# A two-block transformer kernel: what loads and runs behind the first weight units, and a new order in its attention stages

## What is computed

```python
h = rmsnorm(x, attn_norm_g)
qa, ka, va, qb, kb, vb = split(h @ w_in)       # widths 512 128 128 512 512 512
qa = apply_axial_rope(rmsnorm(qa, a_q_norm_g)) # 8 heads of 64
ka = apply_axial_rope(rmsnorm(ka, a_k_norm_g)) # 2 heads of 64
out_a = softmax(qa @ ka.T * scale) @ va        # grouped queries, "a"
qb = rmsnorm(qb, b_q_norm_g); kb = rmsnorm(kb, b_k_norm_g)
p = softmax(qb @ kb.T * scale + rel_bias[bucket])        # 4 heads x 2 parts, "b"
ob = (p[0] - lam * p[1]) @ vb                  # lam from four vectors of 64
x = x + concat(out_a, rmsnorm(ob) * c) @ w_out
x = x + square(relu(rmsnorm(x, mlp_norm_g) @ w_up)) @ w_down
```

## Time and profile before

| | us |
|---|---|
| runs before | 1024.4, 1025.13, 1030.17 (median 1025.13) |
| profiled execution | 1021.25 |
| its span | 1019.9 |
| PE busy in it | 982.2 (96%) |
| DVE busy | 721.9 (71%) |
| ACT busy | 521.2 (51%) |
| POOL busy | 56.8 (6%) |
| granted TensorE clock, mean | 0.99 |

### The profile page before, as it was taken

The page is one execution under the profiler, slowest core; times in us unless marked ns, Lnnn a source line. Parts: engine busy times, 40 slices in busy tenths (PEclk is TensorE's granted clock), DMA queues, the critical chain, the costliest instruction groups (busy, mean ns, idle before and its releaser), DMA issues.

```text
span 1019.9 us, 12867 instructions
## 1 busy us (share of the span) xinstructions
PE 982.2 (96%) x4772; PEld 808.6 (79%) x4772; DVE 721.9 (71%) x1073; ACT 521.2 (51%) x805; POOL 56.8 (6%) x64
## 2 busy tenths in 40 slices
PE   6999789999999999999989999999988989999998
PEld 5877578888888888888878888888877868888887
DVE  4865667889776777777767987797666866656653
ACT  5555555555345544444457755456464564444531
POOL 2211100000000000000000022030100000000000
PEclk7999999999999999999999999999999999999999
DMA  7742237888887688778755766786542628764761
GB/s 242 219 157 81 87 122 235 273 270 290 295 300 275 207 251 257 227 237 294 280 141 180 250 198 191 253 304 213 178 134 103 218 100 269 237 201 135 257 205 52
DMA packets 116204, 214.64 MB, mean 210 GB/s; under 512 B 8786, under 2 KB 16234, under 8 KB 115886
## 3 DMA queue, kind: packets, MB, share of 16 engines
q1 hardware_dynamic: 115790, 213.53, 64.1%
q0 software_dynamic: 64, 0.07, 0.2%
q10 hardware_dynamic: 288, 0.23, 0.1%
HBM read 212.71 MB, written 2.13 MB: 211 GB/s over the span
## 4 chain that ended last, share of the span: by engine, by line
PE 87%; DVE 6%; ACT 2%; DMA 2%; issue 1%; SPq 1%; POOL 0%; ACTq 0%; DVEq 0%
PE ps L1149 26%; PE ps L1151 26%; PE ps L1150 26%; PE ps L1199 3%; PE ps L1241 2%; DVE wlo L1817 2%; PE ps L1274 1%; DMA raw<-in_w_mix 1%; PE ps L1255 1%; DMA early<-in_w_in 1%; PE ps L1177 1%; DVE qkT L2256 1%; ACT fP L1609 1%; PE ps L1339 1%; PE ps L1341 1%
## 5 line engine op out<-in xcount | busy, mean ns | idle before, releaser
L1455 ACT ACTIVATE whi<-raw 128x1024 fp32r<-128x1024 f32 (+1 forms) x306 | 313.5, 1031 | 311.2 <-PE ps L1151 201.0
L1817 DVE TENSOR_TENSOR wlo<-raw,whi 128x1024 fp32r<-128x1024 f32 (+1 forms) x306 | 359.6, 1189 | 115.3 <-ACT whi L1455 113.0
L1149 PE MATMUL ps<-whi,hTh 128*128 128x512 f32 (+1 forms) x832 | 327.5, 394 | 8.4 <-DVE wlo L1817 4.0
L1151 PE MATMUL ps<-whi,hTl 128*128 128x512 f32 (+1 forms) x832 | 317.1, 381 | 0.0
L1150 PE MATMUL ps<-wlo,hTh 128*128 128x512 f32 (+1 forms) x832 | 316.9, 381 | 0.0
L1149 PEld LDWEIGHTS ps<-whi,hTh 128*128 128x128 f32 x832 | 157.2, 189 | 39.0 <-DVE wlo L1817 5.2
L1151 PEld LDWEIGHTS ps<-whi,hTl 128*128 128x128 f32 x832 | 157.1, 189 | 30.9
L1150 PEld LDWEIGHTS ps<-wlo,hTh 128*128 128x128 f32 x832 | 157.6, 189 | 27.5 <-issue 0.5
L2162 DVE SCALAR_TENSOR_TENSOR aacc<-araw,cs,aacc 128x512 f32<-128x512 f32 x126 | 95.1, 754 | 2.5
L2402 POOL TENSOR_TENSOR stat<-stat,mhalf 128x8 f32<-128x8 f32 (+3 forms) x29 | 35.9, 1249 | 639.3 <-DVE stat L1833 471.4
L1149 PE MATMUL ps<-whi,uh_ffn 128*128 128x512 f32 x176 | 69.3, 394 | 0.0
(11 more groups left out here) (244 smaller groups left out, 1071.9 us busy)
## 6 DMA issues: line engine op xcount, KB each, us to landing
raw<-in_ffn_w_in SPq DMA_DIRECT2D x80, 512.0 KB, 4.4
araw<-in_w_ada SPq DMA_DIRECT2D x72, 512.0 KB, 5.0
raw<-in_w_mix SPq DMA_DIRECT2D x64, 512.0 KB, 4.6
raw<-in_ffn_w_out SPq DMA_DIRECT2D x44, 512.0 KB, 4.7
raw<-in_w_up SPq DMA_DIRECT2D x32, 512.0 KB, 4.6
raw<-in_w_down SPq DMA_DIRECT2D x32, 512.0 KB, 5.1
raw<-in_w_out SPq DMA_DIRECT2D x16, 512.0 KB, 3.9
raw<-in_w_in SPq DMA_DIRECT2D x14, 512.0 KB, 6.1
```

The source lines that it names most:

```text
L1149: pe.e.matmul(o, ah, h[:, j, :], start=s0, stop=False, skip_group_check=True)
L1151: r = pe.e.matmul(o, al, h[:, j, :], start=False, stop=s1, skip_group_check=True)
L1455: act.e.activation(uflat(whi, u), uflat(raw, u), ACT.Copy).then_inc(hi.up(u), 1)
L1817: v.tensor_tensor(uflat(wlo, u), uflat(raw, u), uflat(whi, u).bitcast(f32), SUB).then_inc(lo_dve.up(u), 1)
```

## The change

**The start.** `head` takes four units of qa instead of two through tile 0 (`("attn", "first")` is 4, so the four units 0 to 3 and not five), and the turn of tile 1 stands behind the first half unit instead of the second (`("attn", "turn1")` 1 to 0). `qa`'s `gemm` skips four units. The row sums of squares, the scales and the POOL's `setup_rope` now stand behind the second row of half units instead of ahead of it. How far `hi` and `lo` run ahead is reset (`behind0`, `between0`, `between1`, `hold1`, and `LO["begin"]` for the start), which leaves ACT's and DVE's list of the first five units as it was.

**The loads.** The `rope` load leaves ACT's list and the two `gq` loads leave POOL's. All three go to SP, behind unit 7 and ahead of `relb`.

**Attention and mlp.** New LAG numbers move the head norm of qb and of kb ahead on DVE (L1941 to L1956), a transpose group of `nat` ahead on PE, and the second scores group of part b up to the first. In the tail of the attention stage the transposes of `W1` stand one half unit earlier; LO for `mlp` goes from 4 to 2, and the `u` transposes of w_up move. From w_down on PE's list is as before. `row` now waits for a free row buffer, which changes nothing in the lists.

```diff
-LAG = {("attn", "between1"): 4, ("attn", "hold1"): 0, ("attn", "turn1"): 1, ("attn_a", "round"): 24,
...
-       ("attn_a", 5): 1, ("attn_a", 6): 3, ("attn_a", 7): 6, ("attn_a", 8): 3, ("attn_a", 9): 4,
+LAG = {("attn", "behind0"): 5, ("attn", "between0"): 0, ("attn", "between1"): 5, ("attn", "first"): 4,
+       ("attn", "hold1"): 2, ("attn", "turn1"): 0, ("attn_a", "round"): 24, ("attn_a", 0): 1, ("attn_a", 1): 2,
...
-LO = {"attn": 1, "ffn1": 0, "ffn2": 0, "merged": 0, "mix": 4, "mixT": 2, "mlp": 4, "u_ffn1": 3, "u_ffn2": 0,
-      "u_mlp": 0, "y": 3, "yb": 2}
+LO = {"attn": 1, "begin": 0, "ffn1": 0, "ffn2": 0, "merged": 0, "mix": 4, "mixT": 2, "mlp": 2, "u_ffn1": 3,
+      "u_ffn2": 0, "u_mlp": 0, "y": 3, "yb": 2}
...
-            first = blocks[then]["units"][:2 if stage == "attn" else LEAD]
+            first = blocks[then]["units"][:LAG["attn", "first"] if stage == "attn" else LEAD]
...
                 if i == LAG[stage, "turn1"]:
                     turn(stage, 1, lag(stage, "between1", 0))
+            for u in first:
+                half(u, 1)
+                tick()
             if stage == "attn":
                 sums("attn")
                 for t in range(2):
                     order.append(("scale", "attn", t))
                 order.append(("setup", "rope"))
-            for u in first:
-                half(u, 1)
-                tick()
...
-        turn("attn", 0, 1)
+        turn("attn", 0, LAG["attn", "between0"], LAG["attn", "behind0"])
         head("attn", "qa")
-        gemm("qa", skip=2)
+        gemm("qa", skip=LAG["attn", "first"])
...
         act.e.dma_start(colp[:, :], d["colp"]).then_inc(ld_c.up(), 16)
-        act.e.dma_start(rope[:, :, :, :], d["rope"]).then_inc(ld_rope.up(), 16)
...
-        for i, name in enumerate(("a_q_norm_g", "a_k_norm_g")):
-            g.dma_start(gq[:, i, :], rows(d[name], 0, [[1, 64]])).then_inc(ld_gain[i].up(), 16)
         setup_rope()
...
+        q.dma_start(rope[:, :, :, :], d["rope"]).then_inc(ld_rope.up(), 16)
+        for i, name in enumerate(("a_q_norm_g", "a_k_norm_g")):
+            q.dma_start(gq[:, i, :], rows(d[name], 0, [[1, 64]])).then_inc(ld_gain[i].up(), 16)
         q.dma_start(relb[:, :], d["rel_bias"]).then_inc(ld_m.up("relb"), 16)
```

More of the change, by code:

```diff
@@ new lines @@
+LAG = {("attn", "behind0"): 5, ("attn", "between0"): 0, ("attn", "between1"): 5, ("attn", "first"): 4,
+       ("attn", "hold1"): 2, ("attn", "turn1"): 0, ("attn_a", "round"): 24, ("attn_a", 0): 1, ("attn_a", 1): 2,
+       ("attn_a", 10): 2, ("attn_a", 2): 1, ("attn_a", 3): 2, ("attn_a", 4): 3, ("attn_a", 5): 1, ("attn_a", 6): 5,
+       ("attn_a", 7): 4, ("attn_a", 8): 6, ("attn_a", 9): 9, ("attn_b", "round"): 24, ("attn_b", "then"): 24,
+       ("attn_b", "wait"): 22, ("attn_b", 0): 3, ("attn_b", 1): 12, ("attn_b", 2): 13, ("attn_b", 3): 6,
+       ("attn_b", 4): 1, ("attn_b", 5): 21, ("attn_b_t", 1): 3, ("attn_b_t", 2): 14, ("attn_b_t", 3): 8,
+       ("attn_b_t", 4): 10, ("conv", 0): 1, ("conv", 1): 3, ("conv", 2): 4, ("end", "late"): 15,
[3 rows of a table added]
+       ("ffn2", "turn0"): 3, ("ffn2", "turn1"): 2, ("fox", "turn"): 5, ("fox", 0): 2, ("fox", 1): 1, ("fox", 2): 7,
[4 rows of a table added]
+       ("gates", 1): 6, ("gates", 2): 4, ("gates", 3): 9, ("gates", 4): 1, ("glu", "turn"): 5, ("glu", 0): 9,
+       ("heads", "turn"): 6, ("heads", 0): 1, ("heads", 1): 3, ("heads", 2): 9, ("mT", "turn"): 1, ("mT", "wait"): 3,
+       ("mix", "between0"): 0, ("mix", "between1"): 0, ("mix", "hold0"): 4, ("mix", "hold1"): 0, ("mix", "late"): 2,
+       ("mix", "turn0"): 3, ("mix", "turn1"): 1, ("mlp", "between0"): 4, ("mlp", "between1"): 0, ("mlp", "hold0"): 1,
+       ("mlp", "hold1"): 0, ("mlp", "late"): 8, ("mlp", "turn0"): 1, ("mlp", "turn1"): 0, ("mlstm", 0): 9,
+       ("mlstm", 1): 1, ("mlstm", 2): 1, ("o", 0): 2, ("o", 1): 4, ("o", 2): 5, ("rope", "turn"): 1, ("rope", 0): 1,
+       ("rope", 1): 4, ("rope", 2): 1, ("rope", 3): 5, ("sub0", "turn"): 20, ("sub0", "wait"): 2, ("sub0", 0): 15,
[3 rows of a table added]
@@ L408, in plan @@
         jobs, done = [], set()
-        at = {"done": 0, "prep": 0, "tick": 0, "ada": None, "limit": len(units) - 1, "quiet": False, "act": "attn"}
+        at = {"done": 0, "prep": 0, "tick": 0, "ada": None, "limit": len(units) - 1, "quiet": False, "act": "begin"}
         opened, lows = set(), []
@@ L715, in head @@
         def head(stage, then):
-            first = blocks[then]["units"][:2 if stage == "attn" else LEAD]
+            first = blocks[then]["units"][:LAG["attn", "first"] if stage == "attn" else LEAD]
+            assert LAG[stage, "turn1"] < len(first)
             pairs.take(then)
@@ L947, in row @@
         def row(*key):
+            while None not in rowr.held:
+                tick()
             rowr.take(*key)
```

11 lines of the change are left out of this document (removed), and 21 rows, old and new, of the table LAG.

## The result

| | before | changed |
|---|---|---|
| runs of the first comparison | 1024.4 to 1030.17, median 1025.64 (4) | 1011.4 to 1017.79, median 1013.86 (4) |
| runs of the second, on another chip | 1021.4 to 1030.19, median 1027.84 (11) | 1012.22 to 1016.71, median 1015.6 (6) |
| profiled execution | 1021.25 (span 1019.9) | 1015.7 (span 1014.3) |

The changed kernel is faster: the ratio is 0.9881 (95% interval 0.9834 to 0.9928) in the first comparison and 0.9879 (0.9853 to 0.9904) in the second, some 12 us. The direction was right and the size half of what came.

What follows compares the result with a forecast made beforehand. PE was busy 982 of 1019.9 us, leaving its idle time and low-clock matmuls to win. Start 4.6 plus attention 1.0 gave 5.6 us, 1025.1 to 1019.5; range 1015 to 1024.

Steps and rivals of the forecast that it cites:

- Part 3: Start, behind qa: small loads at 2.04 us each make unit 9 land at 26.8, limiting the start's gain to 4.6 us.
- Part 1, d: Start: how much earlier unit 4 lands without rope and gq loads ahead; taken as 2.0 us, bounds 0.5 to 2.8.
- Rival B: Start: unit 4's gain is only the bytes ahead, 0.5 us; 3.8 us gained in all, 1021.3; chance 0.22.
- Part 2: Start: 12 matmuls move into PE's idle time, qa ends 4.4 + d us earlier, or 2.5 + d at the low clock.
- X: Start: gain at PE's end of qa, before any limit by unit 9; 4.5 to 6.4 us with d = 2.
- rival C: Start: unit 9 is not late, so X counts in full; 7.8 us gained in all, 1017.3; chance 0.16.
- A: As rival: the forecast itself, 5.3 to 6.6 us gained, chance 0.43. As trace landmark: the bias table's matmuls on PE.
- Covers: Start: moved loads still land in time, second gq near 18 to 20, POOL's steps end by 24; costs nothing.
- Part 4: Attention: three changed PE waits sum to 1.0 us gained, from −0.5 to +1.7.
- (a): Attention at 65.68: PE's wait for DVE's nat of qb goes, +0.95 us.
- (c): Attention at 92.70: PE's wait for mixTl grows as two nat transpose groups move ahead of its chain, −0.75 us.
- (b): Attention at 110.53: the 1.72 us wait for P goes, the second scores group waits about 0.8; sum +0.8 us.

Runs made afterwards that it cites:

- e5_gq: Kernel before with only the two gq loads moved from POOL to SP behind the eight units; one run, 1019.31 us beside 1022.96 for before.
- e4_order: Kernel before with only the new order of the start, its loads and attention order kept; ratio 0.9941.
- e8_lam: Changed kernel with the four lam loads issued behind unit 9 instead of ahead of unit 8; one run, 1014.24 us.
- e7_pool_late: Changed kernel with both gq loads on POOL's queue again, issued once unit 4 has landed; one run, 1018.12 us beside 1022.96 for before.
- e3_loads: Kernel before with only the rope and two gq loads moved to SP behind unit 7; ratio 0.996.
- e1_start: Changed kernel with the attention and mlp order of before, so only start and loads changed; ratio 0.989, median 1017.08 us against 1026.16.
- e2_attn: Kernel before with only the attention and mlp order of the changed kernel; ratio 0.9976, median 1024.87 us.
- e13_half: Kernel before with one of the two gq loads moved from POOL to SP behind the eight units; one run, 1026.34 us beside a median of 1027.84.
- e12_best: Changed kernel with lam loads behind unit 9 and 6 w_out matmuls between the first two scores groups, 12 behind the second; ratio 0.99, median 1017.22 us.

## Why the forecast was half of what came

The forecast was 5.6 us, and 11.8 and 12.2 came. The step that failed is the price of the small loads ahead of unit 9 (Part 3); the largest misses beside it are the stretch behind part b's scores, which had no term, and a rest that no landmark shows.

**Where tile 1 starts (right).** The first product of tile 1 stayed at unit 4's copy plus 3.04 (12.42 to 15.46), as the prediction had it from 15.13 to 18.16.

**Part 1, d (size).** Taken as 2.0 of a range to 2.8, measured 2.71; e5_gq gives all of it by gq alone. The rows 113.6% against 5.1% were rightly read as gq's doing; nothing in them spoke for staying below the upper bound. Rival B fell.

**Part 2 (right).** 12 matmuls moved into idle time and the clock was up in time: 4.4 + d = 7.1 forecast for that case with the measured d, 6.98 measured; e4_order with the order alone 4.52.

**Part 3, unit 9 (the step that failed).** The prediction priced each gq at 2.04, the spacing of the four `lam`, and had unit 9 land at 26.8; it landed at 22.5, and the start gave 7.0 instead of 4.6. Of these 4.3 us 0.7 are the larger d, and 3.6 the price. Even for a small load with nothing large ahead of it the price was high: e8_lam freed 5 us by moving four, 1.25 each. For one that runs beside the units ahead of it, as both gq do, it was wrong: 0.9 for the two and the tables, where the prediction had 4.5, or 1.8 for the two by e7_pool_late, where it had 4.1. The rows had it: `lam`'s first landed 5.0 us after its issue, at 16.2, in the middle of the weights, and only the later ones spread out. So `min(X, 4.3 to 5.6)` was no bound and X counted in full, as in rival C, which had a chance of 0.16 and should have been as likely as A. Its price, the bytes alone (0.08 us for a gain at 403 GB/s), does not hold either. Whether a unit 9 at 26.8 would have held PE back is untested; no run had it later than 24.3.

**Covers (right in the outcome).** The second gq landed at 15.2 and POOL's `ropeg` was ready at 20, where the same price had put 18 to 20 and 24; the tables came in time, and no wait for them stands in any trace.

**Part 4, attention (right up to the second P transpose in sum, not in its parts).** (a) The 0.95 at 65.68 went, and a new wait of 0.48 and a transpose group took its place: 0.06 net up to 85.67, not 0.95. (c) The lead grew by 0.53 to the first scores, where −0.75 was forecast; the wait there fell from 1.07 to 0.27, with 0.58 ahead of it. (b) The second P transpose's 1.72 went for 0.93 at the scores, 1.0 net of 0.8 forecast. Sum 1.6 for a forecast 1.0, within its range; that the errors of (a) and (c) cancel is luck.

**Behind it (no term).** The prediction had no term for the waits behind the second P transpose, and gave no reason. The wait of 3.31 at 133.63 fell to 0.34 (0.64 in the second trace). How much of such a wait is seen depends on the clock of the half units ahead of it, the stretch as a whole does not: from the first `mixTl` to the second it is 8.63 or 8.64 us in all seven traces of the changed order, with waits from 0.34 to 1.10, and 9.43 to 9.93 in the seven of before's. So this place gives 0.8 to 1.3. By B the order gives 3.3 on the mean of the traces, but 2.8 in the two that were compared first.

**The sum.** 7.0 at A and 3.3 to B are 10.3; the medians differ by 11.8 and 12.2, the second with an interval from 9.9 to 15.1. Of the 6.2 to 6.6 us that the forecast lacked, 2.4 come from unit 9's price and 2.3 from the attention and what lies behind it. The rest, 1.5 to 2, lies within that interval and stays open: no landmark shows it. It may be the clock's. Over the 94 runs of all kernels with four runs or more, 0.001 of mean clock goes with 0.38 us (an estimate, by least squares within each kernel and chip), and at equal mean clock the second comparison comes to 10.4 us. But part of the rise from 0.9805 to 0.9848 is the start, where before's trace has 10 us of low clock and the changed one's 3.6, and that part is in the 10.3 already.

**What the profiled execution hid.** The forecast was made against one execution of 1021.25, and the comparison of the two profiled ones alone (5.6 us, by chance the forecast's number) would have confirmed a wrong sum. The row of stretches from 745 to 785 us tells them apart, before first, then changed:

```profile
745.00:785.00 40.00, 34.34 (x205) 27.75 (x204) 22.26 (x58) 20.56 (x51) 1.09 (x1) 0.96 0.27 90
```

```profile
745.00:785.00 40.00, 36.64 (x178) 31.26 (x179) 21.45 (x56) 18.02 (x47) 1.09 (x1) 0.74 0.19 66
```

No part of the change touches that stretch, and e3_loads, with 0.96 there too, and e1_start, with 0.79, have the same order in it. Still it may not be chance: around there ten of the eleven traces with the start's new order have some 17 us or more of low clock, and four of the six with the old one under 10 (e2_attn has 21, e13_half 14). The unprofiled runs do not bear it out, since their mean clock is the higher one with the change. Both possible causes stay open.

## What to carry to other kernels

Price a load by where it stands in its queue's backlog, and not by how far apart others landed in another stretch: beside bulk transfers a gain cost under 1 us where the spacing said 2, while a run of small broadcast loads with the bulk behind them left the engines all but idle. Keep the first loads from POOL's queue out of the stretch in which the first weights decide the start. Compare traces at landmarks of the same operation, not by their spans, when the clock differs between executions; and treat orders that are tied by counted lags as one setting, since each half undone alone was longer than both kernels.

## What the runs showed of the hardware

- With a single gain load of 33 KB on POOL's queue, q1 got 22.6% of the engines' time from 6 to 7 us and all queues together moved 135 GB/s from 5 to 9 (e13_half); without it they moved 371 (e5_gq). A second such load added nothing (170 and 147 with both). Issued 10 us later, the two took a fifth of the engine time and held up nothing that PE saw (e7_pool_late).
- Four loads of one 256-byte row to 128 partitions, last in the queue ahead of two weight units, left the DMA engines 0.19 busy at 53 GB/s for 4 us; behind the units it was 0.76 and 257 (e8_lam; e12_best 0.72 and 241).
- The granted clock fell to 0.5 (the 1.2 GHz level) in three stretches only, the start, part b of the attention and the second block's attention, each with idle time of PE ahead of it. How much of a stretch it took differed between executions of one program order: A to the second `mixTl` took 104.1 to 104.2 us in three traces of before's order with 3.6 us at the low clock there, and 106.0 to 107.7 in four with 13.8 to 16.8 us.
- In the changed order the stretch from A to B took 494.8 to 495.1 us in seven traces, whether the clock was low for 9.8 or for 14.0 us of the attention: waits for DVE took up all but some 0.2 us of the difference.
